# The third mixer of a two-model kernel as one region of three lanes

## What is computed

```python
def odd_mixer(h, w_in, sinks, w_out, rel_bias):
    rq, rk, rv, rg, sq, sk, sv = split_cols(h @ w_in, ODD_SPLITS)
    y_ret = retention(rq, rk, rv)                        # 4 heads, keys of 128, values of 256
    y_ret = y_ret * silu(rg)
    y_swa = sliding_window_attention(sq, sk, sv, sinks, rel_bias)   # 8 heads of 64, 2 kv heads
    return concatenate([y_ret, y_swa]) @ w_out

def retention(q, k, v):                                  # chunks of 128 tokens, 4 of them
    Q, K = rope(q), rope(k) * 128 ** -0.5
    scores = einsum("bclhd,bcshd->bchls", Q, K) * decay_mat
    inner = scores @ V                                   # within a chunk
    state_prev = scan over chunks of (K * zeta)^T V      # state entering each chunk
    cross = (Q * xi) @ state_prev
    return rms_norm(inner + cross)                       # per head of 256

def sliding_window_attention(q, k, v, sinks, rel_bias):  # a query block sees its own and the one before it
    logits = q k^T / 8 + bias, masked to 0 <= dist < 128
    p = softmax([logits, sink])[..., :-1]
    return p @ v
```

## Time and profile before

| | |
|---|---|
| median of 3 runs | 4137.59 us (4133.99 to 4138.14) |
| profiled execution | 4126.41 us, its span 4124.2 us |
| TensorE busy | 3675.7 us (89%) |
| VectorE, ScalarE, GpSimd busy | 1818.9, 1327.4, 447.3 us |
| the odd mixer | from 1218.8 to 1418.9 us |
| mean granted TensorE clock | 0.914 of full speed |

### The profile page before, as it was taken

How to read it: one execution, slowest core, us unless ns; L and a number is a source line. 1 busy time by engine, 2 the same in 40 slices (tenths; PEclk the granted TensorE clock), 3 DMA queues, 4 the chain that set the end, 5 groups by cost and what they waited for, 6 DMA issues and landing times. The chain is left out here.

```text
span 4124.2 us, 48005 instructions
## 1 busy us (share of the span) xinstructions
PE 3675.7 (89%) x19513; PEld 2799.3 (68%) x19513; DVE 1818.9 (44%) x2862; ACT 1327.4 (32%) x2080; POOL 447.3 (11%) x377
## 2 busy tenths in 40 slices
PE   6988989999985799995998897999978989799998
PEld 5777766888763468883676445788766764377886
DVE  4774655433423443323542443454444424344434
ACT  3422543232313332322321443333333223333333
POOL 0011001200003011100131000210002300003100
PEclk8999999999997699997998878999989969799999
DMA  6641233422210112212210003223131000113230
GB/s 224 201 141 51 68 108 106 170 102 92 82 51 0 61 64 100 94 70 82 67 33 22 1 1 107 87 87 113 41 93 48 21 22 1 64 59 106 84 117 26
DMA packets 229340, 316.20 MB, mean 77 GB/s; under 512 B 13053, under 2 KB 168542, under 8 KB 227590
## 3 DMA queue, kind: packets, MB, share of 16 engines
q1 hardware_dynamic: 229126, 313.18, 22.8%
HBM read 310.52 MB, written 5.26 MB: 77 GB/s over the span
## 5 line engine op out<-in xcount | busy, mean ns | idle before, releaser
L491 PE MATMUL out<-h_lo,w_hi 128*128 128x512 f32 x2608 | 1042.7, 400 | 39.2 <-DVE w_lo L482 35.0
L492 PE MATMUL out<-h_hi,w_hi 128*128 128x512 f32 x2608 | 1021.7, 392 | 0.0
L493 PE MATMUL out<-h_hi,w_lo 128*128 128x512 f32 x2608 | 1021.4, 392 | 0.0
L482 DVE TENSOR_TENSOR w_lo<-ring,w_hi 128x1024 fp32r<-128x1024 f32 (+2 forms) x473 | 581.8, 1236 | 987.0 <-ACT w_hi L477 981.8
L477 ACT ACTIVATE w_hi<-ring 128x1024 fp32r<-128x1024 f32 (+2 forms) x473 | 483.3, 1028 | 1168.3 <-PE out L493 1078.4
L491 PEld LDWEIGHTS out<-h_lo,w_hi 128*128 128x128 f32 x2608 | 493.7, 189 | 163.2 <-issue 47.0
L492 PEld LDWEIGHTS out<-h_hi,w_hi 128*128 128x128 f32 x2608 | 493.6, 189 | 112.2 <-issue 11.0
L493 PEld LDWEIGHTS out<-h_hi,w_lo 128*128 128x128 f32 x2608 | 493.3, 189 | 104.0
L491 PE MATMUL item_banks<-h_lo,w_hi 128*128 128x512 f32 (+1 forms) x696 | 315.8, 454 | 14.4 <-DVE w_lo L482 5.1
L492 PE MATMUL item_banks<-h_hi,w_hi 128*128 128x512 f32 (+1 forms) x696 | 277.9, 399 | 0.0
L493 PE MATMUL item_banks<-h_hi,w_lo 128*128 128x512 f32 (+1 forms) x696 | 277.7, 399 | 0.0
(11 more groups left out here) (489 smaller groups left out, 4775.4 us busy)
## 6 DMA issues: line engine op xcount, KB each, us to landing
ring<-in_mlp_w SPq DMA_DIRECT2D x30, 2048.0 KB, 8.0
ring<-in_w_up SPq DMA_DIRECT2D x44, 1024.0 KB, 6.5
tiles<-in_mod_w SPq DMA_DIRECT2D x80, 512.0 KB, 4.6
ring<-in_e_w_in SPq DMA_DIRECT2D x48, 512.0 KB, 4.2
ring<-in_w_in SPq DMA_DIRECT2D x22, 1024.0 KB, 5.2
ring<-in_w_down SPq DMA_DIRECT2D x10, 2048.0 KB, 7.7
ring<-in_o_w_in SPq DMA_DIRECT2D x7, 2048.0 KB, 7.8
tiles<-in_mod_w SPq DMA_DIRECT2D x8, 1024.0 KB, 8.7
```

The source lines that it names most:

```text
L482: return nc.vector.tensor_tensor(lo.bitcast(F32R), x, hi, ALU.subtract)
L491: nc.tensor.matmul(out, wh, xl, start=start, stop=False, **kw)
L492: nc.tensor.matmul(out, wh, xh, start=False, stop=False, **kw)
L493: return nc.tensor.matmul(out, wl, xh, start=False, stop=stop, **kw)
```

## The change

- **The odd mixer is one region.** Three lanes, `turn_lane`, `retention_lane` and `window_lane`, and a small one for the table. The loops are unrolled, so nothing is copied to fixed places: products read `qkT`, `v_rows`, `sk_dup` and `sv_rows` directly.
- **Retention**: per chunk of 128 tokens, in two halves of two heads, with the squares, sums, root, scaling and gating of that chunk behind it. The first chunk has no cross part, the last none of the state's work. Due times begin at 14.5 with rounds of 17.5 us.
- **Sliding attention**: a batch is one head pair with all its four query blocks. The comparison with the sink, its exponential, the sum and the reciprocal are done once a batch, on 8 columns; transposes and copies take both heads of a query block. Due times begin at 1.0 with rounds of 19.0 us.
- **The gate's SiLU** moves to `even_tail`: the eight tiles that ScalarE and VectorE copied out in turns are all taken out by ScalarE with SiLU.
- **Cosines and sines** are loaded in the closing lane of `even_tail`, into two tiles that are free by then. Also there: the load of ScalarE's exponential table.
- **A second set of bias rows**: the opening makes `window_rows` in DRAM, of 384 columns a row and with the mask of the window in it, so that the mixer need not add the mask.

The diff, cut to its core:

```diff
@@ opening
-    values = scratch[0:HEADS, at + 2 * S:at + 3 * S + P]
+    values, near = scratch[0:HEADS, at + 2 * S:at + 3 * S + P], scratch[0:HEADS, 6 * D:6 * D + BAND + P]
...
                 if c == 6:
                     sp.wait_ge(values_out, 1)
-                    sp.wait_ge(masked, 1)
+                    sp.wait_ge(masked, 2)
+                    sp.wait_ge(near_out, 1)
                     sp.dma_start(value_rows.ap(), values).then_inc(values_kept, 16)
+                    sp.dma_start(near_rows.ap(), near).then_inc(values_kept, 16)
...
             sp.dma_start(k.bias_rows.ap(), value_rows.ap().unsqueeze(1).to_broadcast([HEADS, P, S + P])).then_inc(bias_kept, 16)
+            sp.dma_start(k.window_rows.ap(), near_rows.ap().unsqueeze(1).to_broadcast([HEADS, P, BAND + P])).then_inc(bias_kept, 16)
...
             nc.vector.tensor_copy(values[:, 0:S], banks[0:HEADS, 6, :]).then_inc(values_out, 1)
+            dve.wait_ge(masked, 2)
+            nc.vector.tensor_copy(near[:, P:2 * P], banks[0:HEADS, 6, S - P:S]).then_inc(near_out, 1)
@@ even_tail
-        ins += [up(O_RG + t * COLS, feat(gT, 4 * t)) for t in range(2)]
+        ins += [up(O_RG + t * COLS, lambda e, j, ps, t=t: nc.scalar.activation(gT[:, 4 * t + j, :], ps, ACT.Silu), owner="act") for t in range(2)]
...
+        @closing.sync
+        def _(sp):
+            sp.wait_ge(mlp_done, DT)
+            sp.dma_start(tiles[:, 24:26, :], a["ret_table"][:, 0:2 * S].rearrange("p (f n) -> p f n", f=2)).then_inc(turns_in, 16)
+            sp.wait_ge(turns_in, 16)
+            yield 1.0
+
+        @closing.scalar
+        def _(act):
+            nc.scalar.preload_act_table_set(EXP_LN_SET)
+            yield 1.0
@@ turn_lane: GpSimd and VectorE, tile j
+            yield STEP_T * j + 1.0
+            pool.wait_ge(swap_done, j + 1)
+            nc.gpsimd.tensor_tensor(qkT[:, j, :], qkT[:, j, :], cos, ALU.mult).then_inc(cos_done, 1)
...
+                yield STEP_T * (j - 1) + 2.3
+                dve.wait_ge(cos_done, j)
@@ retention_lane: TensorE
+            at = BEGIN + ROUND * c
+            yield at
+            if c == 0:
+                pe.wait_ge(rotated, 2 * H)
...
+            for u, first, begin in halves(c):
+                yield begin + 3.0
...
+            yield at + 12.0
+            pe.wait_ge(squared, c + 1)
...
+            for h in range(H):
+                for e in range(2):
+                    last = nc.tensor.matmul(turned[:, h * P:(h + 1) * P], k.at["ones"], sq[:, 2 * h + e, :], start=(e == 0), stop=(e == 1))
@@ window_lane: SP, TensorE, GpSimd
+        yield -1.0
+        sp.dma_start(band[:, 0:2, :], bias_window(k.window_rows, 0, 2, 0, BAND, BAND + P)).then_inc(first_in, 16)
+        sp.dma_start(sinks[:, :], a["o_sinks"][0].partition_broadcast(P)).then_inc(sinks_in, 16)
+        sp.dma_start(band[:, 2:HEADS, :], bias_window(k.window_rows, 2, HEADS - 2, 0, BAND, BAND + P)).then_inc(band_in, 16)
...
+        steps = [(when, what, i, s) for i in range(PAIRS) for s in range(TC)
+                 for when, what in ((step_time(i, s), "score"), (step_time(i, 0) + 16.6 + 1.5 * s, "turn"), (step_time(i, 0) + 19.0 + 1.5 * s, "mix"))]
...
+        yield 0.0
+        pool.wait_ge(sinks_in, 16)
+        nc.gpsimd.tensor_scalar(neg_sinks[:, :], sinks[:, :], -1.0, None, ALU.mult).then_inc(sinks_turned, 1)
@@ odd_mixer
+    with Region(k) as r:
+        banks = r.psum("odd_banks", [P, 8, S])
...
+            sp.dma_start(table[:, :], a["ret_table"][:, 2 * S:]).then_inc(table_in, 16)
+
+        rotated, cos_done = turn_lane(k, r, r.lane(0.0, 1.0), qkT, tiles[:, 24, :], tiles[:, 25, :], banks[:, 4:6, :], 1.5)
+        retention_lane(k, r, r.lane(0.0, 1.0), qkT, v_rows, gT, table, table_in, retention_constants()[1], rotated, banks[:, 4:8, :], 14.5, 17.5)
+        window_lane(k, r, r.lane(0.0, 1.0), a, tiles[:, 28:32, :], sk_dup, sv_rows, gT[:, DT:, :], cos_done, banks[:, 0:4, :], 1.0, 19.0)
```

More of the change, by code:

```diff
@@ L1258, in __init__ @@
         self.length = self.quarter * self.quarters
-        self.begin = 0.0
+        self.begin, self.owner = 0.0, owner
         self.frees = []
@@ new lines, in _ @@
+    @lane.vector
+    def _(dve):
+        for j in range(2 * RET_H + 1):
+            if j < 2 * RET_H:
+                yield STEP_T * j + 1.0
+                dve.wait_ge(swap_done, j + 1)
+                if j >= 2:
+                    dve.wait_ge(rotated, j - 1)
+                nc.vector.tensor_tensor(crossed[:, j % 2, :], banks[:, j % 2, :], sin, ALU.mult).then_inc(cross_done, 1)
+            if j:
+                yield STEP_T * (j - 1) + 2.3
+                dve.wait_ge(cos_done, j)
+                dve.wait_ge(cross_done, j)
+                nc.vector.tensor_tensor(qkT[:, j - 1, :], qkT[:, j - 1, :], crossed[:, (j - 1) % 2, :], ALU.add).then_inc(rotated, 1)
@@ L1945, in _ @@
                 pe.wait_ge(scored, c + 1)
-                pe.wait_ge(xi_done, c + 1)
-                pe.wait_ge(chunk_out, c + 1)
-                for h in range(H):
-                    for e in range(2):
-                        to = out_ps[:, 2 * h + e, :]
-                        nc.tensor.matmul(to, v_c[:, h, e * P:(e + 1) * P], scores[:, h, :], start=True, stop=False)
-                        last = nc.tensor.matmul(to, state[:, h, e * P:(e + 1) * P], q_xi[:, h, :], start=False, stop=True)
+                if c:
+                    pe.wait_ge(xi_done, c)
+                    pe.wait_ge(state_done, (c - 1) * H + first + 2)
@@ new lines, in _ @@
+                if 2 * c + u >= 1:
+                    pe.wait_ge(out_left, 2 * c + u)
+                for h in range(first, first + 2):
+                    for e in range(2):
+                        to = out_ps[:, (2 * (h - first) + e) * P:(2 * (h - first) + e + 1) * P]
+                        last = nc.tensor.matmul(to, v_rows[:, c, h * RET_V + e * P:h * RET_V + (e + 1) * P], scores[:, c % 2, h, :],
+                                                start=True, stop=(c == 0))
+                        if c:
+                            last = nc.tensor.matmul(to, state[:, h, e * P:(e + 1) * P], q_xi[:, c % 2, h, :], start=False, stop=True)
@@ new lines, in _ @@
+    @lane.scalar
+    def _(act):
+        for c in range(TC):
+            at = BEGIN + ROUND * c
+            for u, first, begin in halves(c):
+                yield begin + 5.2
+                act.wait_ge(out_done, 2 * c + u + 1)
+                if c >= 2 and u == 0:
+                    act.wait_ge(gated, c - 1)
+                nc.scalar.activation(out[:, c % 2, 4 * u:4 * u + 4, :], out_ps.rearrange("p (j n) -> p j n", j=4), ACT.Copy).then_inc(out_left, 1)
+            yield at + 10.0
+            act.wait_ge(out_left, 2 * c + 2)
+            if c:
+                act.wait_ge(stat_done, c)
+            nc.scalar.activation(sq[:, :, :], out[:, c % 2, :, :], ACT.Square).then_inc(squared, 1)
+            yield at + 14.0
+            act.wait_ge(stat_done, c + 1)
+            if c:
+                act.wait_ge(normed, c)
+            flat = rstd[:, :, :].rearrange("p h n -> p (h n)")
+            inverse_root(k, act, flat, flat, turned, 1.0 / RET_V, log_done, c + 1).then_inc(rstd_done, 1)
@@ new lines, in _ @@
+    @lane.gpsimd
+    def _(pool):
+        for c in range(TC):
+            at = BEGIN + ROUND * c
+            if c:
+                yield at - 1.0
+                if c == 1:
+                    pool.wait_ge(table_in, 16)
+                    pool.wait_ge(rotated, 2 * H)
+                if c >= 3:
+                    pool.wait_ge(out_done, 2 * c - 2)
+                nc.gpsimd.tensor_tensor(q_xi[:, c % 2, :, :], qkT[:, 0:H, here(c)], xi, ALU.mult).then_inc(xi_done, 1)
+            yield at + 17.5
+            pool.wait_ge(normed, c + 1)
+            nc.gpsimd.tensor_tensor(gT[:, 0:2 * H, here(c)], out[:, c % 2, :, :], gT[:, 0:2 * H, here(c)], ALU.mult).then_inc(gated, 1)
```

532 lines of the change are left out of this document (235 added, 297 removed).

## The result

The changed kernel took **4040.26 us** in the median of 4 runs (4034.31 to 4044.3) against 4135.95 for the kernel before in the same comparison (4 runs): a ratio of 0.9768, 95% interval 0.9756 to 0.9781. The forecast was 4043.7, range 4023 to 4076. The sum came out; three of its terms did not: the region's start and the loss in its steady part were set 5 and 17 us too low, TensorE's need 11 us too high. The region is 11 us longer than forecast, and a gain of about the same size that nobody forecast, outside the stretches that were sized, covers it.

The account below looks back on a forecast made before the run. In the odd mixer nothing is full; a chain through all engines sets its 200.1 us. The sum -200.1 + 1.2 (borders) + 100 (region) + 5.0 (opening) = -93.9, from 4137.6, gave 4043.7 us, range 4023 to 4076.

Parts of the forecast that it names:

- the region's start: Mixer region up to retention's first scores: 18.5 to 19 us where due at 14.5, cosines waiting behind the sinks' negation.
- the loss in its steady part: Region after 18.5 us: 7% for waits and 2% for clock on 68.4 us, giving 74.5, then 7 of tail.
- TensorE's need: TensorE's work in the region: 80 us at 2.4 GHz: sliding 43, retention 30.3, rotation 7.0.
- The opening: Kernel's opening: the `window_rows` spread delays the first weights 4.7 us, 5.0 with the copy; range 0.3 to 8.5.
- My own sign of failure: Steady part: prediction wrong if TensorE idles over 10 us because of a chain called covered (a batch's exponentials, a chunk's root).
- Region: Whole odd mixer as one region: 18.5 + 74.5 + 7 = 100 us, with 1.2 us at the borders besides; bounds 88 and 112.
- 20% of loss: Region's upper bound: 20% of loss instead of 9, with the start's bound of 7, gives 112 us.
- The due times hold: Rival for the region: waits hidden, region ends at 88 to 90 us, 11 less, time 4033; chance 0.14.
- The clock stays at 1.2 GHz: Rival for the region: TensorE stays at half clock, region about 150 us, time 4094; chance 0.07.
- its half share: Half of the slow-clock rival: clock low in a few stretches, stretching the range upward to 4076.
- In a row: Rival for the region: lanes run one after another, region 202 us, 8 us slower, time 4146; chance 0.02.

Follow-up runs that it names:

- again: The changed kernel, unaltered, run and profiled again on the same chip as the combined edits: 4043.68 us, ratio 0.9781, region 110.0 us.
- the run with the lanes in a row: Changed kernel with the sliding lane's due times 94 us later (`BEGIN` 95.0 instead of 1.0): 4090.82 us, region 156.6 us.
- together, filled: Changed kernel with respread opening, `q_xi` before gate, norm behind scores, late sinks and table, plus unread TensorE products in idle pieces: 4033.6 us, ratio 0.9752.
- the three unchanged regions: Regions of the changed kernel, its repeat, and it with spreads 128 outermost: 112.2, 110.0, 109.4 us; times 4040.3, 4043.7, 4038.2 us.
- With filling: Changed kernel with 8 unread 128x512 TensorE products ahead of the outputs of chunks 1, 2 and 3: 4039.2 us, ratio 0.9769.

## Why the prediction came out, point by point

- **The opening: right in cause and size, not in every part.** 5.0 were forecast, 5.14 measured at the first split (57.36 against 52.22), and the form of the spread is the cause. But the share of 0.5 went on only until 51 us (54 expected), and 1.74 us of later issue by SP, which the forecast had at nothing, came beside it; how the two add up is not shown. That the mixer started 8.95 us later in this profile is 5 of the opening and 4 of scatter; again it was 6.2.
- **The start: too short by 5 us.** The rotation's end was forecast at 18 and the first scores at 18.5; both came at 23.7. GpSimd's first product did start at 5.3 (5.25 measured) behind the negation. What failed is "with the steps between, at 18": the old stage's 17.7 us had rotation alone. Now VectorE has the shifts in the same queue, the first of them 2.56 us in wait for the band; its additions take 1.04 us in the mean, up to 1.74 beside GpSimd's products, where 0.67 is their shortest; and the first batch's two 8-column operations, ahead of the last sums, take 1.25 and 1.19 us beside the same products. In the run with the lanes in a row, without the shifts, the rotation was done after 19.0 us for the same late beginning.
- **TensorE's need: too high by 11 us.** 80 us at full clock forecast, 68.7 measured; in the steady part 57.0 instead of 68.4. The term that was mis-sized is the sliding lane's: 43 us forecast, at most 30.8 measured (11.6 + 10.0 + 9.2 in the rows of "together, filled"), while what remains, 37.9, fits the 37.3 forecast for retention and rotation. The 43 came from half of a cold unit and a tenth for waits. But half of the cold time was not the hot time: the 64 instructions of the scores took 31.8 us before, at a mean clock of 0.53, and 11.6 here at 0.98. Before, they stood in twos, now four and more follow each other; that this makes the difference is argued, not shown.
- **The loss in the steady part: too low by 17 us.** 6.1 us of waits and clock and 7 of tail forecast, together 13; measured 9.0 of cold clock and 21.1 idle, 30. I took the even mixer's 7% for waits from a lane that is woven with dense projections, where every wait finds other work. Here both chains pass through the same two queues: the gate ahead of `q_xi`, and the norm ahead of the scores. The text of the lane shows it; I read the due times and not the order in which a lane emits. My own sign of failure, over 10 us idle in the steady part, came true, though by another chain than those I named.
- **Region: 101.2 forecast, 112.2 and 110.0 measured**, 5 and 17 us too little, 11 too much. It lies at the bound of 112, for which "20% of loss" and 7 of start were meant.
- **Why the sum was right all the same.** By its parts it should be -200.1 + 110.5 + 5.1 = -84.5 (mean of the three unchanged regions), and the medians of the two comparisons are 95.7 and 93.1 apart. So 9 to 11 us of the gain in the medians lie outside the stretches that I sized. Put otherwise: from the profiled execution the measured parts give 4126.4 - 84.5 = 4041.9, which is the changed kernel's time; the forecast took off 9.4 us too much and added 11.2 for the distance of that execution from its median, and the two cancel. That is luck. Where the 9 to 11 us lie is not settled. The part behind the mixer took 2705.3 and 2712.5 us in two profiles with the old mixer and 2703.1 in the mean of twelve with the new one, which points there, but with two profiles against a scatter of 20 us it is argued, not shown.
- **The rivals.** "The due times hold" (88 to 90) needed warm and ordered lanes: 95.1 is the nearest that any version came. "The clock stays at 1.2 GHz" fell as a whole (0.85), but its half share was real: in the steady part the clock was to be over 0.9 and TensorE busy for over 85%; it was 0.85 and 76%. "In a row" did not happen, and its price was too high: 156.6 measured, in the run made for it, instead of 202.

## What to carry to other kernels

In a woven region write down, for each engine, the order of the instructions of different lanes, and ask of each one that waits what stands behind it: a due time doesn't reorder a lane's own text. An idle piece of 4 to 5 us on TensorE can cost more than its length, here 13.9 idle and 9.0 us of half clock, and an edit that shortens it may show little until the neighbouring wait goes too, here 2.0 us and then 7.7. Price thin products by ones that ran at the same clock and as densely, not by half of cold and lonely ones. When single edits are smaller than the scatter of the time, measure them by their own stretch and compare the combination.

## What the runs showed of the hardware

- A VectorE operation on 8 columns with both inputs in SBUF lasted as long as the GpSimd product beside it, 2.33 us instead of 0.17. With `q_xi` early, where only the scores behind it held TensorE, that wait was 3.68 us and the two others 1.86 and 1.48.
- The spread with 8 outermost also held its issuer: 4.70 us on SP against 0.68 with 128 outermost.
- TensorE's granted clock fell from 1.00 to 0.50 by the end of each of three idle pieces of 4.3 to 5.0 us, and stayed at 0.50 from 1276 to 1280 us though TensorE was busy without a gap again (4.00 of 4.00 us). With filling it stayed at 1.00 for over 70 us.
